# Five chunk pairs of each panel with seven products instead of four, over seven slots for split weights instead of eight

## The reference

```python
f = rmsnorm(h, g_ffn[i])
h = h + (jax.nn.silu(f @ w_gate[i]) * (f @ w_up[i])) @ w_down[i]
gte = jax.nn.sigmoid(rmsnorm(h, g_ple[i]) @ w_pgate[i] + b_pgate[i])
h = h + (p[i] @ w_ple[i]) * gte
return rmsnorm(h, g_final)
```

## Time and profile before

| what | value |
|---|---|
| median of 3 runs | 1162.54 us (1162.49 to 1162.54) |
| the profiled execution's own time | 1162.51 us |
| its span, from the first to the last instruction | 1160.7 us |
| mean granted TensorE clock | 0.998 of full speed |
| busy in the span: PE, PEld, DVE, ACT, POOL | 1147.6, 968.9, 945.9, 630.8, 124.8 us |
| DMA, mean over the span | 192 GB/s |

### The profile page before, as it was taken

The page is one execution under the profiler, slowest core; times in us unless marked ns, Lnnn a source line. Parts: engine busy times, 40 slices in busy tenths (PEclk is TensorE's granted clock), DMA queues, the critical chain, the costliest instruction groups (busy, mean ns, idle before and its releaser), DMA issues.

```text
span 1160.7 us, 16347 instructions
## 1 busy us (share of the span) xinstructions
PE 1147.6 (99%) x5618; PEld 968.9 (83%) x5618; DVE 945.9 (81%) x1272; ACT 630.8 (54%) x809; POOL 124.8 (11%) x74
## 2 busy tenths in 40 slices
PE   9999999999999999999999999999999999999996
PEld 8889989988888877888888888888888888888886
DVE  6689767767777999988989898989989898947674
ACT  6544465466455664746556464647364555647552
POOL 0222443436031000000000000000000000000111
PEclk9999999999999999999999999999999999999999
DMA  9655555454655565664747474745647374754541
GB/s 343 215 182 181 182 182 165 163 179 149 198 170 177 181 237 199 200 234 145 254 143 254 143 253 145 253 162 200 216 153 262 128 272 140 250 201 153 201 160 73
DMA packets 113121, 223.38 MB, mean 192 GB/s; under 512 B 5194, under 2 KB 6418, under 8 KB 112817
## 3 DMA queue, kind: packets, MB, share of 16 engines
q1 hardware_dynamic: 112608, 222.08, 56.4%
q10 hardware_dynamic: 464, 0.66, 0.2%
HBM read 220.63 MB, written 2.10 MB: 192 GB/s over the span
## 4 chain that ended last, share of the span: by engine, by line
PE 92%; DVE 3%; issue 2%; ACT 1%; POOL 1%; POOLq 0%; DVEq 0%; ACTq 0%
PE ps L1423 14%; PE ps L1425 14%; PE ps L1424 14%; PE ps L1626 11%; PE ps L1628 11%; PE ps L1627 11%; PE ps L1457 3%; PE ps L1456 3%; PE ps L1455 3%; PE ps L1465 2%; PE ps L1621 1%; PE ps L1620 1%; PE ps L1619 1%; DVE w_lo L950 1%; PE ps L1432 1%
## 5 line engine op out<-in xcount | busy, mean ns | idle before, releaser
L655 ACT ACTIVATE w_hi<-w_raw 128x1024 fp32r<-128x1024 f32 (+1 forms) x286 | 291.2, 1027 | 272.5 <-PE ps L1425 154.1
L950 DVE TENSOR_TENSOR w_lo<-w_raw,w_hi 128x1024 fp32r<-128x1024 f32 x250 | 301.0, 1216 | 118.5 <-ACT w_hi L655 117.0
L1423 PE MATMUL ps<-w_hi,oT_hi 128*128 128x512 f32 x320 | 125.7, 393 | 0.0
L1425 PE MATMUL ps<-w_hi,oT_lo 128*128 128x512 f32 x320 | 124.6, 390 | 0.0
L1424 PE MATMUL ps<-w_lo,oT_hi 128*128 128x512 f32 x320 | 124.6, 389 | 0.0
L1423 PE MATMUL ps<-w_hi,nT_hi 128*128 128x512 f32 x280 | 111.4, 398 | 0.0
L1425 PE MATMUL ps<-w_hi,nT_lo 128*128 128x512 f32 x280 | 109.2, 390 | 0.0
L1424 PE MATMUL ps<-w_lo,nT_hi 128*128 128x512 f32 x280 | 109.0, 389 | 0.0
L579 POOL TENSOR_TENSOR w_lo<-w_raw,w_hi 128x1024 fp32r<-128x1024 f32 x36 | 86.4, 2399 | 182.3 <-ACT w_hi L655 182.3
L1006 DVE SCALAR_TENSOR_TENSOR ps<-arena,taps,ps 128x256 f32<-128x256 f32 x232 | 94.7, 482 | 0.2 <-ACT ps L776 0.2
L1626 PE MATMUL ps<-w_hi,nT_hi 128*128 128x512 f32 x220 | 86.5, 393 | 0.0
(11 more groups left out here) (278 smaller groups left out, 2579.8 us busy)
## 6 DMA issues: line engine op xcount, KB each, us to landing
w_raw<-in_w_gate SPq DMA_DIRECT2D x88, 512.0 KB, 3.9
w_raw<-in_w_up SPq DMA_DIRECT2D x88, 512.0 KB, 4.8
w_raw<-in_w_down SPq DMA_DIRECT2D x44, 1024.0 KB, 5.1
w_raw<-in_w_in SPq DMA_DIRECT2D x32, 1024.0 KB, 5.1
w_raw<-in_w_out SPq DMA_DIRECT2D x16, 1024.0 KB, 5.0
w_raw<-in_w_pgate SPq DMA_DIRECT2D x16, 1024.0 KB, 5.0
w_raw<-in_w_in SPq DMA_DIRECT2D x14, 512.0 KB, 10.2
w_raw<-in_w_ple SPq DMA_DIRECT2D x2, 1024.0 KB, 6.8
```

Of the source, the lines that this page charges most:

```text
L655: nc.scalar.activation(tiles_of(m)[0], source_of(m), ACT.Copy).then_inc(hi_ready, 1)
L950: nc.vector.tensor_tensor(lo, source_of(m), hi.bitcast(F32), ALU.subtract).then_inc(lo_ready, 1)
L1423: nc.tensor.matmul(banks[t][:, :], x_hi[:, k, rows], hi[:, k], start=start, stop=False)
L1425: ins = nc.tensor.matmul(banks[t][:, :], x_lo[:, k, rows], hi[:, k], start=False, stop=stop)
```

## The change

`QUAD_KINDS` becomes `PPSSSSSP`: pair 4, plain before, is now a Strassen pair, so five of them (pairs 2 to 6) stand in a row. A panel has 26 units of gate and up and 8 of down, 34 in all. The fifth pair's activation sums take the place of what was the fifth slot (part of `oT`), so seven slots are left. 34 is no multiple of 7, so the slots start again at slot 0 with each panel: units 0 to 5 of a panel lie where units 28 to 33 of the one before lay, 6 units back, and unit 6 where unit 27 lay, 13 back (`slot_back`). The panel's units from 7 on wait for the unit 7 back. ACT and DVE split unit t + 7 in step t.

```diff
-QUAD_KINDS = "PPSSPSSP"
+QUAD_KINDS = "PPSSSSSP"
...
-LOOP_SLOTS = 8
+LOOP_SLOTS = 7
...
-                n = (m - LOOP0) % LOOP_SLOTS
+                n = (m - LOOP0) % PER_LOOP % LOOP_SLOTS
                 if n == 4:
-                    return tuple(o[:, 12:16].rearrange("p (k a) t -> p k (a t)", k=2) for o in (oT_hi, oT_lo))
-                if n == 5:
                     return w_more[:, 0:2], w_more[:, 2:4]
-                if n >= 6:
-                    return w_extra[:, n - 6, 0:2], w_extra[:, n - 6, 2:4]
+                if n > 4:
+                    return w_extra[:, n - 5, 0:2], w_extra[:, n - 5, 2:4]
...
+        def slot_back(m):
+
+            j = (m - LOOP0) % PER_LOOP
+            if j >= LOOP_SLOTS:
+                return LOOP_SLOTS
+            return PER_LOOP - max(k for k in range(PER_LOOP) if k % LOOP_SLOTS == j) + j
...
             elif in_loop(m) and m >= LOOP0 + LOOP_SLOTS:
-                engine.wait_ge(half_done, m - LOOP_SLOTS + 1 + PER_LOOP * it)
+                engine.wait_ge(half_done, m - slot_back(m) + 1 + PER_LOOP * it)
             elif PLE0 <= m < PLE0 + SLOTS:
-                engine.wait_ge(half_done, m - LOOP_SLOTS + 1)
+                engine.wait_ge(half_done, m - PER_LOOP % LOOP_SLOTS + 1)
```

## The result

The changed kernel takes 1213.38 us (median of 4 runs, 1213.17 to 1213.44) against 1162.53 for the kernel before: 50.9 us or 4.4% slower, ratio 1.0438 (95% interval 1.0425 to 1.0451). The forecast was 1208.1, the range 1186 to 1218.

A forecast was written before the change was run, and what follows sets the result against it. PE was taken to set the steady panel's pace, DVE close behind. Block products saved, the run's loss and the add waits summed to +45.6 us on 1160.7, so 1206.3, and 1208.1 with 1.8 around it; range 1186 to 1218.

The forecast's parts named there:

- PE work removed: On PE, a fifth Strassen pair saves one block product per panel: 0.68 us, 6.8 us over ten panels.
- DVE work added: On DVE, the fifth Strassen pair adds 4.3 us per panel, making 61.3 of 62.8 us, counted from start to start.
- The run of five: Five Strassen pairs in a row: DVE falls behind and PE waits three times in the fifth, 1.6 us a panel.
- the rivals with one cost alone (1173 and 1190): Only the run of five costs: 1173 us, chance 0.07; only the panel step costs: 1190 us, chance 0.08.
- The step from panel to panel: Steps 27 to 32: down adds behind splits that wait one unit longer stop PE, 1.20 us three times a panel.
- It is just free: At step 27's split, DVE finishes earlier work at 51.7 us, just before the slot releases it at 52.1.
- Four activation sums ... none on PE: Ahead of the loop, extra sums and splits cost DVE at most 1.7 us, first panel 0.35 us later, PE nothing.
- The sum: Whole span: first panel +6.0, panels two to nine +36.3, last +3.3, together +45.6 us on 1160.7.
- The first panel itself: First panel, where DVE never catches up and the three add waits follow: +6.0 us.
- The rival in which the short gaps bring the clock down: Matmuls between the first and third add wait run at 1.2 GHz: 10.9 us more per panel, near 1313, chance 0.03.

The follow-up runs named there:

- the last kernel: The changed kernel with adds ahead of the held splits, a second place for the weight sums (pair 4's in step 3) and the third activation-sum group later: 1159.23 us.
- both kernels with a wait of 2.76 us: The changed kernel with a second place for weight sums and pair 4's sums in step 3, 1196.76 us; the same with early adds and later activation sums, 1159.23 us.

## Why the prediction was right, point by point

**PE work removed**, 0.68 us a panel: right, 0.68 in the last kernel's steady panels.

**DVE work added**, 4.3 us a panel: right, 61.41 busy for the 61.3 counted. Counting DVE from start to start was right as well: from the first sum of the third pair of the run to that of the fourth the changed kernel's DVE took 622.11 - 615.51 = 6.60 us against my 6.59, with DVE always at work. The sum of whole durations was 6.9, and the trace doesn't agree with it. The prediction gave only half of what the Trainium skill, "VectorE: DVE Perf Modes", The DRAIN you can't avoid, says; the same paragraph ends: "A next op that is not held starts earlier". The trace agrees with that, 1.14 us apart at 1.22 us each.

**The run of five**, 1.6 us: 1.74 measured. In steady panels units 20, 21 and 22 waited and the units ahead of them did not, as worked out, and DVE's timeline has no idle time from unit 10's split to the step 27 split. Moving sums into the idle time took this amount away (1.76), and one more instruction of 0.61 us gave 0.58 us a panel. That the run's cost and the step's cost are separate, against the rivals with one cost alone (1173 and 1190), is shown by the runs that took away each alone.

**The step from panel to panel**, 1.20 us three times: 1.27 measured. The mechanism is shown from both sides: the adds moved ahead of the splits gave back 36.8 us (29 x 1.27 = 36.8), and the wait alone put 26.5 us on the kernel before, which the same move took away again. "It is just free" was right as well, by 0.28 us where I had 0.4. But with a free slot the first add would have been about 0.7 us late all the same, so at this add the backlog from the run is a second cause, which the prediction did not name. In the kernel before with the longer wait DVE stood idle for 2.08 us ahead of that split, so there the wait alone made the add late. The size was off by 0.07 because I took PE's restart from one row of the first panel, 0.06 us behind the add's end; in steady panels it is 654.49 - 654.35 = 0.14 (more on this in the last section).

**"Four activation sums ... none on PE"** is the step that failed, and the largest part of the error after the adds. I let DVE's waits at the end of the stretch ahead of the loop cover 1.7 us that falls earlier, where DVE has no idle time at all. PE waited 1.36 us for the next low split, and the loop began at 389.94 instead of 388.30: 1.6 us lost. When the third group moved to just ahead of the idle time the wait was 0.42 us, the loop began at 388.96 and the whole time fell by 1.4 us. The 0.42 us that stayed are open.

**The sum.** Forecast +45.6, measured +50.9. Eight steady panels gave 8 x 4.85 = 38.8 for 36.3, the start 1.6 for nothing. The first panel itself lost 6.35 (73.00 against 66.65) for 6.0, and the last 3.9 for 3.3.

**Clock.** The changed kernel's granted clock was 1.00 in every panel, with six waits in a steady one and twelve in the first. The rival in which the short gaps bring the clock down did not happen. The Trainium skill, "TensorE: Matmul & The Clock Gate", A second HAM failure mode, tells of such gaps making the clock swing; these, of up to 1.36 us, did not. Behind a longer one it fell: both kernels with a wait of 2.76 us have a stretch at 0.50 behind it.

## What to carry to other kernels

When a ring of buffers loses a slot or restarts out of step, don't ask only whether the data still come in time: look at what stands behind the lengthened wait in that engine's order, and who waits for it. Here the splits were in time and the adds behind them cost 36.8 us, which a change of one step in the order gave back. An engine at 61 of 63 us fits on average and still costs time where its work bunches; the cure was to fill its idle time just ahead of the bunch, with a second place for the data, not to take work away. In the first panel, where there was no idle time to fill, the same move made a wait of 2.8 us, and the clock fell behind it. And cover must be found at the place where the work falls: idle time ten us later hides nothing.

## What had not been expected of the hardware

PE restarts at two distances behind the add that it waits for, and which one depends on the panel. In the changed kernel's first and last panel, whose instructions are written out, it is 0.06 us (the last: the add starts at 1063.23 and takes 1.28, PE restarts at 1064.57). In panels that the engines run as a loop it is 0.13 to 0.14 (994.68 and 1.28, 996.09; 654.35, 654.49). The last panel's first unit lies between, 0.10 behind its add (1008.11 and 1.28, 1009.49). The timelines show the same in their idle times, 0.95 against 0.97. Waits in the loop are against a value that depends on the turn; whether that is the cause was not tried.

Behind each such wait the unit takes 2.86 us in place of 2.72, in the changed kernel as in the row of before. The shortest seen, 0.16 us ahead of unit 0 in the kernel before with the longer wait, has it too. A wait thus costs 0.14 us more than it lasts, and the three short waits in the run, in which PE starts 0.3 to 0.6 us late (0.16 to 0.41 in the brackets), are worth counting one by one.
